# Two transformer blocks in split fp32r: the first feed-forward product partly by seven block products for eight

## The reference, cut to what matters

```python
D_MODEL = 2048; SEQ = 256; D_FF = 4 * D_MODEL

def squared_relu_mlp(h, w1, w2):
    z = jax.nn.relu(h @ w1)        # 256x2048 @ 2048x8192
    return (z * z) @ w2            # 256x8192 @ 8192x2048
...
    x = x + squared_relu_mlp(rms_norm(x, ffn_norm[i]), w_ff1[i], w_ff2[i])
```

## Time and profile before

| what | value |
|---|---|
| time, median of 3 runs | 2984.85 us (2984.52 to 2986.6) |
| span of the profiled execution (its own time beside the runs) | 2982.6 us |
| TensorE (PE) busy, of which weight loads | 2945.8 us (99%), PEld 2425.4 us |
| VectorE (DVE) busy | 1853.8 us (62%) |
| ScalarE (ACT) busy | 1493.9 us (50%) |
| GpSimd (POOL) busy | 635.6 us (21%) |
| DMA | 611.34 MB, mean 205 GB/s |

### The profile page before, as it was taken

One profiled execution on the slowest core, in us unless ns is written; L12 is line 12 of the kernel. 1 busy time (PEld: TensorE's weight loads), 2 busy tenths in 40 slices (PEclk: granted clock), 3 DMA queues, 4 the chain that ended last, 5 costly groups with the idle time before them and its releaser, 6 DMA issues.

```text
span 2982.6 us, 37047 instructions
## 1 busy us (share of the span) xinstructions
PE 2945.8 (99%) x13140; PEld 2425.4 (81%) x13140; DVE 1853.8 (62%) x2485; ACT 1493.9 (50%) x2004; POOL 635.6 (21%) x1257
## 2 busy tenths in 40 slices
PE   8999999999999999999999999999999999999998
PEld 7888888888888778788888888888888887878887
DVE  6537655546565777876555555556557777887555
ACT  6435444444344666655434444345444546775433
POOL 0003302213034210013303122133323673110210
PEclk9999999999999999999999999999999999999999
DMA  7546666666667655556666666676866786666774
GB/s 261 169 150 206 209 214 197 217 198 215 193 200 237 209 180 159 166 168 216 212 199 211 201 206 205 198 219 209 246 204 205 216 241 184 208 203 210 247 254 156
DMA packets 338542, 611.34 MB, mean 205 GB/s; under 512 B 37473, under 2 KB 62433, under 8 KB 337633
## 3 DMA queue, kind: packets, MB, share of 16 engines
q1 hardware_dynamic: 293392, 541.13, 58.1%
q0 software_dynamic: 44432, 67.45, 7.2%
q10 hardware_dynamic: 576, 0.94, 0.1%
HBM read 561.15 MB, written 10.49 MB: 192 GB/s over the span
## 4 chain that ended last, share of the span: by engine, by line
PE 87%; DVE 7%; ACT 3%; issue 1%; DMA 1%; DVEq 0%; ACTq 0%
PE acc L1935 28%; PE acc L1937 28%; PE acc L1936 28%; DVE wlo L1349 2%; DVE wlo L1344 1%; ACT whi L1016 1%; PE tp L2105 1%; DVE ob L1724 0%; PE sd L1999 0%; PE sd L2024 0%; DMA raw<-in_w_mem_kv 0%; PE tp L2095 0%; PE tp L1953 0%; ACT whi L1019 0%; PE tp L2055 0%
## 5 line engine op out<-in xcount | busy, mean ns | idle before, releaser
L1935 PE MATMUL acc<-whi,set_hi 128*128 128x512 f32 x4080 | 1607.5, 394 | 15.0 <-DVE wlo L1349 9.6
L1937 PE MATMUL acc<-whi,set_lo 128*128 128x512 f32 x4080 | 1589.3, 390 | 0.0
L1936 PE MATMUL acc<-wlo,set_hi 128*128 128x512 f32 x4080 | 1588.6, 389 | 0.0
L1349 DVE TENSOR_TENSOR wlo<-raw,whi 128x1024 fp32r<-128x1024 f32 x944 | 1133.4, 1220 | 711.9 <-ACT whi L1016 710.3
L1016 ACT ACTIVATE whi<-raw 128x1024 fp32r<-128x1024 f32 x944 | 981.7, 1058 | 926.4 <-PE acc L1937 659.3
L1935 PEld LDWEIGHTS acc<-whi,set_hi 128*128 128x128 f32 x4080 | 766.3, 188 | 190.9 <-DVE wlo L1349 18.2
L1937 PEld LDWEIGHTS acc<-whi,set_lo 128*128 128x128 f32 x4080 | 766.0, 188 | 161.6
L1936 PEld LDWEIGHTS acc<-wlo,set_hi 128*128 128x128 f32 x4080 | 766.5, 188 | 157.7 <-issue 1.9
L983 POOL DMA_DIRECT2D u<-u x832 | 407.6, 498 | 1470.0 <-DVE u L1472 1379.6
L1344 DVE SCALAR_TENSOR_TENSOR wlo<-raw,par,whi 128x512 fp32r<-128x512 f32 x160 | 111.6, 746 | 47.1 <-ACT whi L1019 46.4
L1019 ACT ACTIVATE whi<-raw,par 128x512 fp32r<-128x512 f32 x160 | 104.3, 715 | 22.6 <-PE acc L1937 11.2
(11 more groups left out here) (276 smaller groups left out, 1274.1 us busy)
## 6 DMA issues: line engine op xcount, KB each, us to landing
raw<-in_w_ff SPq DMA_DIRECT2D x512, 512.0 KB, 4.5
raw<-in_w_in SPq DMA_DIRECT2D x248, 512.0 KB, 4.5
raw<-in_w_out SPq DMA_DIRECT2D x96, 512.0 KB, 4.4
u<-u POOLq DMA_DIRECT2D x832, 32.0 KB, 4.6
raw<-in_w_mem_kv SPq DMA_DIRECT2D x32, 512.0 KB, 4.7
raw<-in_w_proj_a SPq DMA_DIRECT2D x32, 512.0 KB, 4.4
raw<-in_w_proj_b SPq DMA_DIRECT2D x32, 512.0 KB, 6.7
raw<-in_w_kv SPq DMA_DIRECT2D x48, 256.0 KB, 3.3
```

What stands on the lines that cost most here:

```text
L1349: V.tensor_tensor(wlo[:, c], raw[:, c], whi[:, c].bitcast(f32), ALU.subtract).then_inc(w_lo, 1)
L1935: T.matmul(o, h[:, tok], whi[:, c], start=first, stop=False)
L1936: T.matmul(o, h[:, tok], wlo[:, c], start=False, stop=False)
L1937: ins = T.matmul(o, l[:, tok], whi[:, c], start=False, stop=last)
```

## The change

In chunks 2 to 4 of each layer (three chunks, two layers: six pairs) the first two of the four column groups of the first product are no longer computed slab by slab. Tokens are halved (128 each), K is halved and the two groups are the two column halves; the 2 by 2 block product is made with seven block products (p1 to p7) instead of eight, in a Winograd form. Each is 128 tokens by K = 1024 by 512 columns: four part slabs of six matmuls.

- The sums of token blocks are made once a layer, in the first chunk (`sum_full`, `sum_`, `sum_hi`, `sum_lo`).
- The sums of weight blocks are made anew for each pair, all by VectorE: p1's four blocks are loaded into `chain_raw`, and a running sum over p1, p5, p6, p4 adds the next block into it (`chain_sum`); p7 takes `chain_raw - raw` (`u3`). So 16 of a pair's 28 parts have a sum ahead of their split. Blocks of weights are loaded again for each product, 28 loads for 16.
- The 28 parts of a pair are put into the stream one behind each slab, from slab 8 of the preceding chunk's second product (START = 8): parts stand behind slabs 8 to 35, where slab 32 is the first of the next chunk. `sum`s stand two tasks ahead in VectorE's queue.
- The products are combined from four single banks of PSUM (halves of `tp` and `sd`) by `part_p1`, `part_p5`, `part_c11`, `part_q`, `part_n2`, `part_p7`, `part_n1`; relu, square, turn and tail follow, at the places shown below.
- The hardware loops are gone: every engine's queue is written out task by task.

The diff, cut to its core:

```diff
+STAGES = ("p1", "p2", "p5", "p3", "p6", "p7", "p4")
+CHAIN = {"p1": 0, "p5": 1, "p6": 2, "p4": 3}
+QUARTERS = NK // 2 // SLAB_K
+START = 8
...
+        for c in range(NCHUNK):
+            halved = c > 0
+            gs = [sc.group(f"w_ff1{layer}", 0, D * c + GW * i, a) for i in range(2 if halved else 0, 4)]
+            if c == 0:
+                sc.fed_late(gs[0])
+                for n in range(4):
+                    sc.at("dve", S * gs[0] + 9 + n, "sum_full", n, sc.tails)
+                for n in range(5):
+                    sc.at("dve", S * gs[0] + 14 + 2 * n, "sum", n)
+                for n in range(4):
+                    sc.at("act", S * gs[0] + (15, 17, 21, 23)[n], "sum_hi", layer, n)
+                    sc.at("dve", S * gs[0] + (17, 19, 23, 25)[n], "sum_lo", layer, n)
             else:
+                v = S * gs[0]
+                for of, kt, add, relu, square, split in (("n2", 0, 0, 1, 2, 6), ("n1", 4, 4, 5, 6, 11)):
+                    sc.at("dve", v + add, "part_" + of, p)
+                    sc.at("act", v + relu, "relu_" + of, p, rst)
+                    sc.at("dve", v + square, "part_square", p, of, sc.staged, sc.tails)
+                    sc.turned(v + square, v + split, ("staged", sc.staged), z, kt)
+                    sc.staged += 1
+                    if of == "n2":
+                        sc.at("act", v + 3, "part_p7", p, sc.staged)
+            for i, g in enumerate(gs):
+                turn = S * (g + 1) + (3 if halved and i == 0 else 1)
+                sc.at("act", S * (g + 1) + 1, "epi_relu2", g, rst, sc.staged, sc.tails)
+                sc.at("dve", turn, "epi_relu2", g, rst, sc.staged, sc.tails)
+                sc.turned(turn, S * (g + 2) + 1, ("staged", sc.staged), z, 4 * i + (8 if halved else 0))
+                sc.staged += 1
+            fs = [sc.group(f"w_ff2{layer}", D * c, GW * i, z) for i in range(4)]
+            sc.weave(fs[0], fs[1], FF2_PAIR)
+            if c < NCHUNK - 1:
+                v = S * fs[0] + START
+                p = sc.pair_of(layer, c + 1, a, v)
+                sc.at("act", v + 6, "part_p1", p)
+                sc.at("act", v + 14, "part_p5", p)
+                sc.at("dve", v + 9, "part_c11", p)
+                sc.at("dve", v + 21, "part_q", p)
...
+            def chain_sum(task):
+                c = slice(task.slot * SLAB, (task.slot + 1) * SLAB)
+                t = chain_raw[task.part.j]
+                dve.wait_ge(ld[task.slot], 16 * task.loads)
+                dve.wait_ge(*(chained(task.part, "p1")))
+                V.tensor_tensor(t, t, raw[:, c], ALU.add).then_inc(sm["chain_add"], 1)
...
+            def part_n2(p):
+                dve.wait_ge(mm, sc.pairs[p].last("p7"))
+                dve.wait_ge(sm["part_q"], p + 1)
+                V.tensor_tensor(stage_a[:, 0:GW], bank_d, mixed_c[:], ALU.add)
+                V.tensor_tensor(stage_a[:, GW:2 * GW], bank_b, mixed_c[:], ALU.add).then_inc(sm["part_n2"], 1)
+
+            def part_n1(p):
+                dve.wait_ge(mm, sc.pairs[p].last("p4"))
+                dve.wait_ge(sm["part_p7"], p + 1)
+                t = stage_a[:, GW:2 * GW]
+                V.tensor_tensor(t, bank_a, t, ALU.add).then_inc(sm["part_n1"], 1)
...
+            for task in sc.stream:
+                lo(task, None if task.part else sc.groups[task.g].fold)
+                ahead = sc.stream[task.n + 2] if task.n + 2 < len(sc.stream) else task
+                if ahead.part and ahead.part.stage == "p7":
+                    u3(ahead)
+                elif ahead.part and ahead.part.stage in ("p5", "p6", "p4"):
+                    chain_sum(ahead)
+                if not task.part:
+                    run(S * task.g + task.s)
...
+            def part_slab(task):
+                part = task.part
+                p, stage = part.pair, part.stage
...
+                pe.wait_ge(w_lo, task.n + 1)
...
+                for t, c in rows_of(task.slot):
+                    h, l = factor(part, part.j * SLAB_K + t)
+                    first = fresh and part.j == 0 and t == 0
+                    last = part.j == QUARTERS - 1 and t == SLAB_K - 1
+                    T.matmul(bank, h, whi[:, c], start=first, stop=False, skip_group_check=True)
+                    T.matmul(bank, h, wlo[:, c], start=False, stop=False, skip_group_check=True)
+                    ins = T.matmul(bank, l, whi[:, c], start=False, stop=last, skip_group_check=True)
+                ins.then_inc(mm, 1)
```

More of the change, by code:

```diff
@@ L60 @@
 NCON = CR2 + 2 * TB * ROPE2
[L63 to L80, removed]
 def at_least_one(n):
-    return (n.base if isinstance(n, N) else n) > 0
+    return n > 0
 def at(n):
-    v = n.v if isinstance(n, N) else n
-    assert not isinstance(v, int) or v > 0
-    return v
+    assert n > 0
+    return n
 class Group:
@@ L102, in __init__, with last @@
         self.need = {}
+class Task:
+    def __init__(self, n, g=None, s=None, part=None):
+        self.n, self.g, self.s, self.part = n, g, s, part
+        self.slot = n % RAW
+        self.loads = 0
+class Part:
+    def __init__(self, pair, stage, j, v):
+        self.pair, self.stage, self.j, self.v = pair, stage, j, v
+        self.n = None
+class Pair:
+    def __init__(self, layer, chunk, src, first):
+        self.layer, self.chunk, self.src, self.first = layer, chunk, src, first
+        self.parts = {}
+    def last(self, stage):
+        return self.parts[stage, QUARTERS - 1].n + 1
 class Schedule:
@@ L119, in __init__, with pair_of, number_all, done @@
         self.norms = 0
-        self.loops = {}
+        self.parts = {}
+        self.pairs = []
+        self.stream = []
+    def pair_of(self, layer, chunk, src, v):
+        p = len(self.pairs)
+        pair = Pair(layer, chunk, src, not any(q.layer == layer for q in self.pairs))
+        self.pairs.append(pair)
+        for i, (stage, j) in enumerate(itertools.product(STAGES, range(QUARTERS))):
+            part = Part(p, stage, j, v + i)
+            pair.parts[stage, j] = part
+            self.parts.setdefault(v + i, []).append(part)
+        return p
+    def number_all(self):
+        taken = [0] * RAW
+        for v in range(NSLAB * len(self.groups)):
+            for part in [None] + self.parts.get(v, []):
+                t = Task(len(self.stream), v // NSLAB, v % NSLAB, part)
+                if part is None:
+                    of, _, _, _ = self.slab_of(t.g, t.s)
+                    taken[t.slot] += SLAB_K if self.groups[of].pieces else 1
+                else:
+                    part.n = t.n
+                    taken[t.slot] += part.stage != "p1"
+                t.loads = taken[t.slot]
+                self.stream.append(t)
+        self.number = {NSLAB * t.g + t.s: t.n for t in self.stream if t.part is None}
+    def done(self, v):
+        return self.number[v - 1] + 1
     def group(self, *a, **k):
@@ L335, in ffn @@
     def ffn(layer, rst, a, z, next_rst, next_gain):
[L337 to L355, removed]
@@ L566, in build @@
                           for n, at in (("set2_hi", place["x"]), ("set2_lo", place["u"]))))
+        at_ = [place["kv"][0] + 4 * NK // 2 * P * i for i in range(6)]
+        at_ += [place["u"][0] + 4 * NK // 2 * P * i for i in (2, 3)]
+        assert at_[5] + 4 * NK // 2 * P == place["kv"][1] and at_[7] + 4 * NK // 2 * P == place["u"][1]
+        sums = [tuple(nc.alloc_sbuf_tensor_at(f"sum{i}_{n}", [P, NK // 2 * P], f32r, offset=at_[2 * i + h])
+                      for h, n in enumerate(("hi", "lo"))) for i in range(4)]
+        chain_raw = [qk[:], prob[:], mkv[:, 0:SLAB], mkv[:, SLAB:2 * SLAB]]
+        first_c, mixed_c = ob, scan
         poolm = kv[:, 0:8 * TOK]
@@ L713, in gout @@
         def gout(g):
[L715 to L716 removed]
+            return out_of[g % 2], g // 2 + 1
         def headwise(kind, i):
@@ L746, in inverse_roots, with block_of, chained, in_rows @@
             return rqs[:, 48 + 8 * i:48 + 8 * (i + 1)] if kind == "mq" else nrs[:, 0:n]
[L748 to L774, removed]
+        def block_of(part, stage):
+            k, n = BLOCKS[stage]
+            pair = sc.pairs[part.pair]
+            row, col = P * (k * NK // 2 + SLAB_K * part.j), D * pair.chunk + GW * (1 - n)
+            return W[f"w_ff1{pair.layer}"][row:row + SLAB_K * P, col:col + GW].rearrange("(t p) n -> p t n", p=P)
+        def chained(part, stage):
+            if stage == "p1":
+                return sm[f"chain_in{part.j}"], 16 * (part.pair + 1)
+            return sm["chain_add"], QUARTERS * (3 * part.pair + CHAIN[stage] - 1) + part.j + 1
+        def in_rows(t):
+            return t.rearrange("p (t n) -> p t n", t=SLAB_K)
         def ut_tiles(kt, n):
@@ L817, in _, with slab @@
         def _(sp):
[L818 to L829, removed]
+            def slab(task):
+                of, k, _, _ = sc.slab_of(task.g, task.s)
+                of = sc.groups[of]
+                if task.n >= RAW:
+                    sp.wait_ge(w_lo, task.n + 1 - RAW)
```

(52 more changed lines are left out.)

317 lines of the change are left out of this document (178 added, 139 removed).

## The result

The changed kernel takes **3034.35 us** (median of 4 runs, 3033.22 to 3035.82) against 2984.68 us before in the same comparison: ratio 1.0166, interval 1.0152 to 1.018. It is slower by 50 us, although it does 144 large matmuls fewer. The forecast was 3050, range 2990 to 3085.

What follows compares the result with a forecast made beforehand. TensorE was taken as the bound, its matmuls time gained while other engines keep supplying slabs. 2982.6 - 32.7 (saving) + 83 (links) + 7 (late starts) + 8 (clock) = 3048 us span, so 3050 us median; range 2990 to 3085.

Steps and rivals of the forecast that it cites:

- The saving, 32.7 us: Six pairs save 144 large matmuls on TensorE at 0.227 us each: 32.7 us.
- From Z to the first turn, 12.2 us: Z is TensorE's start of slab 32, the next chunk's first; VectorE's queued work ends the first turn 12.2 us later.
- The links, 83 us: Turn, shuffle, tail, square, next turn: 18.3 us each, three a pair up to slab 50; 13.9 us lost a pair, 83 for six.
- GpSimd's late starts, 7 us: GpSimd starts 1 in 8 of the 18 shuffles that count 3.1 us late: 7 us (0 to 20).
- The clock, 8 us: TensorE's clock halves after the 4.7 us stop before slab 44: six times 1.3, 8 us (0 or 16 possible).
- The alternating stretch at nothing: Rounds of one slab and one part, 4.09 us each: VectorE's added splits and sums barely fit, cost nothing.
- The cover I named, a lead of 2.9 us: While parts and slabs alternate, a slab is ready about 2.9 us ahead of TensorE; gone with loads of 6 us.
- The stops at slabs 33 to 35, 3.7 us a pair: After the parts' end, TensorE waits for VectorE's delayed splits: some 3.7 us of the 13.9 lost a pair.
- where I had named 80: Sign in the profile after: TensorE's idle time put down to VectorE's splits near 80 us instead of 9.6.
- The hidden shuffle: Rival: VectorE keeps its lead, shuffle and tail stay hidden; 2974 us, or 2952 with the parts' end hidden too; chance 0.15.
- the feed as the bound: Rival: weight loads of 6 us stretch the rounds, 29 us more, 3079 us; chance 0.12.
- "Half hidden": Rival: half of the links' cost is hidden by a lead at turns; about no change to +15 us; chance 0.08.

Runs made afterwards that it cites:

- nosum: Kernel late without the sixteen weight sums of a pair by VectorE, parts split straight from what was loaded: 2954.21 us, ratio 0.9897 to the kernel before.
- plain: Changed kernel's written-out queues without pairs, parts or sums: 2984.26 us, ratio 0.9999 to the kernel before.
- more: Changed kernel with eight more 32 KB DMAs issued by GpSimd ahead of each of 18 shuffles on the links: 3106.2 us, ratio 1.0403 to the kernel before.
- late: Changed kernel with turns, squares and tails moved apart and second product's K tiles ordered 0-3, 4-5, 6-7: 2975.8 us, ratio 0.9967 to the kernel before.
- early: Changed kernel with parts four slabs earlier (START = 4), turns and tails apart, K tiles ordered as in late: 2964.17 us, ratio 0.9932 to the kernel before.

## Why the prediction was right, and what was mis-sized

- **The saving, 32.7 us: right.** nosum, whose links are apart, gets 29.9 of it. The written-out queues cost nothing (plain).
- **From Z to the first turn, 12.2 us: right.** VectorE saw p7's end at 485.57 and ended the turn at 497.28: 11.7 us. From Z by TensorE's starts it is 11.9 in five pairs and 12.5 in one.
- **The links, 83 us: right in place, too large in size.** Turn to turn was put at 18.3 us from the waits of the earlier trace rows. Where GpSimd wasn't late it was 15.6 to 18.8; the second pair's three links are 53.2 us together (682.90 to 736.08) for 54.9, and over the six pairs, late starts taken out, the mean is 52.8. The term that was too large is the shuffle: from GpSimd's start to set_hi it took 10.2 to 13.4 us in the 18 links, 12.25 in the mean, instead of 12.9. With the first turns, the links account for 69 us instead of 83.
- **GpSimd's late starts, 7 us: right.** Two of the 18 shuffles (518.64 and 886.44) came some 3 us late: 6 us. With the 69 these are the 75.5 us from Z to slab 50.
- **The clock, 8 us: about half of it counted, and not where I put it.** The clock fell more often than I took: ten times, after TensorE had idled 1.80 to 4.92 us. But until slab 50 the path runs through VectorE, ScalarE and GpSimd; matmuls at half clock between two late tails only shorten TensorE's next wait. The run more shows it: 6.8 us more of slow matmuls there, and no more time than the links explain. What is slow from slab 50 on does count: 4.1 us in the changed kernel.
- **The alternating stretch at nothing: 4.0 us over six pairs.** Few stops are visible there (0.41 us before the start at 428.12). But the sums did wait for their loads (8 to 10 us for each of the three groups of L1448, 14.7 us for L1440), so VectorE came to p7's end with less lead than I had: it waited 5.2 us there over six pairs. The cover I named, a lead of 2.9 us, was mostly gone.
- **The stops at slabs 33 to 35, 3.7 us a pair: right.** In the changed kernel they are part of the chain and not lost twice. With the links apart they are what remains: in late 3.1 to 3.6 us a pair from Z to slab 50. nosum shows that the sums in VectorE's seven instructions make them.
- **The sum.** The forecast had 83 + 7 + 8 = 98 us of loss, the trace has 69 + 6 + 4 + 4, some 84. So the span came out 14 us below the 3048: 14 by the links, 4 by the clock and 1 by the late starts, less 4 in the alternating stretch. The median lies 2 us lower still against the forecast, because the profiled execution was the longest of the four. By the waits TensorE's matmuls waited 60.6 us for splits, where I had named 80.
- **The rivals.** The hidden shuffle is ruled out by more, the feed as the bound by late. "Half hidden" didn't occur. The rule of the Trainium skill (TensorE: Matmul & The Clock Gate, the table on why this matters for your kernels) that idle gaps between bursts halve the clock: the trace agrees, and the clock fell even after shorter gaps than the page warns of (1.80 and 1.96 us). The cost that I derived from it held only from slab 50 on, for the reason given.

What stays open: early is 13 us above 2951.4. By TensorE's starts 9.4 us of it lie in the 18 slabs and four parts behind p7's end. In its trace TensorE's matmuls waited 2.7 us more for splits than before (12.3 for 9.6) and its weight loads 8.8 us more (27.0 for 18.2); which of VectorE's sums or loads are behind them wasn't tried.

## What to carry to other kernels

A bound engine's time can be cut only as long as its suppliers run ahead; if a step with a round trip through another engine (turn, shuffle, tail) stands in the same in-order queue as the supply, the distance between its two ends must be at least the round trip plus everything queued with it, and taking matmuls away shortens that distance. Before removing work from the busiest engine, write down such round trips with their spans in slabs, and move their ends: here moving places in the queues (from the changed kernel to early) turned 50 us slower into 20 us faster. And as long as a chain through other engines sets the time, don't add what the idle engine loses, its clock included: it is already in the wait. Only what is still slow when the chain has ended is added.

## What the hardware showed that I hadn't expected

- The granted clock fell to half at each of the eight stops in which TensorE idled 2.34 us or more. Of the shorter ones two were also followed by a fall (1.80 us, on at 736.70; 1.96 us, on at 2042.09) and two nearly equal ones weren't (1.99 us, on at 718.25; 1.71 us, on at 1679.28). The length of the last stop alone doesn't tell which.
- The three links weren't equal: the middle one was as short as 15.6 us (shuffles starting at 1644.74 and 1660.30), although the sixteen issues took 7.83 us each time. From GpSimd's start to set_hi it took 10.2 us there and up to 13.4 in a third link (903.55), so the time from the last issue to the last landing varied. What it depends on wasn't tried.
- GpSimd stopped for 6.6 to 7.5 us in the midst of three of the longer trains of DMAs (run more), and started some 3 us late on 2 of 18 shuffles of the changed kernel, each time with nothing awaited that the profile shows.
